# Layer 1 of a two-block transformer kernel: memory heads first, gate panels last, the gates' sigmoid from Exp, Ln and Exp

## The chip, the core and the metric

The kernel runs on one core of a Trainium2 chip. The metric is the device time of one execution in microseconds (us). Five engines work from queues of their own, each strictly in program order: TensorE (PE in the profile, with its weight loads as PEld), VectorE (DVE), ScalarE (ACT), GpSimd (POOL) and SyncE (SP), which issues the loads. They meet at semaphores: an instruction whose wait is not met holds up everything behind it on its engine.

## What is computed

Two blocks run one after the other on 256 tokens of width 1024. The first block has two layers; the change concerns the second of them, layer 1: differential attention over six heads, attention to a memory of 256 rows over four heads, a silu gate on each, and an output projection. All is float32.

```python
h = rms_norm(x, pre_norm[1])
mem_n = rms_norm(mem, mem_norm[1])
k_sh, v_sh = jnp.split(rms_norm(x, kv_norm) @ w_kv, 2, axis=-1)
proj = h @ b_w_in[0]
q, gate, q_mem, g_mem = jnp.split(proj, [BR_W, 2 * BR_W, 2 * BR_W + MEM_W], axis=-1)
# differential attention, per head of 2 x 64 (q, k) and 128 (v)
s = jnp.where(allowed, q @ k.T + bias, -jnp.inf)            # two score maps
attn = softmax(s)[0] - lam * softmax(s)[1]
y_br = rms_norm(attn @ v, subln) * (1.0 - lam_init)
# memory attention, four heads of 64
y_mem = softmax(q_mem @ k_mem.T * 64 ** -0.5) @ v_mem
y = jnp.concatenate([y_br * silu(gate), y_mem * silu(g_mem)], axis=-1) @ w_out[1]
x = x + rms_norm(y, post_norm[1])
```

Then the second block follows (a feed-forward, a mixer with retention and sparse attention, another feed-forward), which the change leaves as it is.

## The kernel before

Activations lie feature-major, in tiles of 128 features by 256 tokens. Weights stream from HBM in panels of 1024 x 128 (one output tile). For float32 accuracy each panel is split: ScalarE copies it to a rounded high part `wh` (step `w_hi`, L1684), VectorE subtracts to get the low part `wl` (step `w_lo`, L2058), and TensorE makes 24 matmuls of 256 columns (L2625, L2626, L2628: high by high, high by low, low by high, for eight slices of 128 features). The inputs are split in the same way into `xh` and `xl` (or `kh` and `kl`).

The function `schedule` makes one list of steps, and each engine's program walks that list and issues its own part of each step. So the order of the list is the order of every queue. `weight_order` fixes the order in which panels are loaded and used; up to five panels are split ahead of their use in this layer. `project` puts a panel's matmuls in the list and keeps its evacuation (for layer 1 the step `proj1` on VectorE, L2331, which multiplies the bank by the row norm and writes `qT`, `kT`, `qm1`, `gm1` or `gate1`) until after the next panel's matmuls; `settle` and `need` put it there at once.

Layer 1 has 28 panels before its output projection: six for q, six for the gate, two for the memory's query (`b_w_in` 12, 13), two for the memory's gate (14, 15), and twelve for k and v (`w_kv`). `LAYER1_BETWEEN` lists most of them in order, and `fill` takes the next one whenever an attention step leaves room. The attention itself is written as streams that `skewed` starts one behind the other:

- `diff_head(h)`, six of them. TensorE makes the scores (step `dif_s_mm`, L2928); VectorE adds the distance bias and takes maxima (`dif_s`, L2356 to L2360); ScalarE takes the Exp with its sums (L1931) and VectorE scales and combines the two maps (`dif_p`, L2366 to L2377); TensorE turns the result (`dif_t`, L2936) and ScalarE copies it; TensorE multiplies with the values (`dif_o`, L2943) and ScalarE squares it (L1943); TensorE sums the squares (`dif_n`, L2610), ScalarE takes Ln and Exp (L1669, L1671) and VectorE writes the head's output `rh` (L2384).
- `memory_stream(j)`, two of them, each with two heads: scores (`mem_s`, L2880), maxima on VectorE (`mem_a`, L2256, L2260), Exp on ScalarE (L1855), normalisation on VectorE (`mem_p`, L2266, L2270), turns on TensorE (`mem_b`, L2891) with copies on ScalarE (L1862), and the product with the values (`mem_c`, L2901), which VectorE multiplies with the gate (L2278).

Before the change the memory streams come after the six heads. The first of them also issues the gates: for the two `gm1` and the six `gate1` tiles ScalarE's Sigmoid (L1675, with a table load, L1662, ahead of it) and GpSimd's product with the gate itself (L1631). Then the step `branch` for each of the six tiles multiplies `rh` with the gate (VectorE, L2292), copies the high part (ScalarE, L1882) and subtracts the low part (VectorE, L2296); the output projection begins with these six slices for its first two panels (L2642 to L2646, `mm_group`), stops for `mem_c` and the two memory tiles, and ends with their two slices. `ln_tables` loads the table of Exp and Ln again. `mix_out` runs the other six panels; the first of them starts at L2625.

## Time and profile before

| | |
|---|---|
| median of three runs | 1252.0 us (1248.49 to 1253.15) |
| the profiled execution | 1251.89 us, of which its span is 1250.1 us |
| mean granted TensorE clock | 0.978 of full speed |
| TensorE busy | 1173.2 us, 94% of the span |
| VectorE, ScalarE, GpSimd busy | 68%, 50%, 15% |
| the chain that ended last | PE 81%, DVE 11%, ACT 5% |
| layer 1 in the span | from about 256 us to about 425 us |

All times below are us from the start of the span. A timeline row gives the start, the busy time, the engine, the line, what is written and read, and in brackets how long the engine sat idle before it and who released it. TensorE's matmuls are pipelined, so a row's time is longer than its distance to the next row. Operands named `bank` are in PSUM; `ta` holds constant tables, among them the identity for turns.

### The profile page before, as it was taken

The page shows a single profiled execution, that of the slowest core. Times are in us where ns is not written, and L with a number is a line of the kernel's source. Part 1 is how long each engine was busy: PE and PEld are TensorE (multiplying, and loading weights), DVE is VectorE, ACT ScalarE, POOL GpSimd, SP SyncE. Part 2 cuts the span into 40 slices and gives each one's busy share as a digit, 9 for nine tenths or more (in the row PEclk, how much of TensorE's full clock was granted, in tenths as well). Part 3 has the DMA queues.
Part 4 walks back from the last instruction along what each step waited for, and adds up shares of the span by engine and source line. Part 5 has one row for each costly group of instructions (what it writes and reads, how often), then busy time and mean ns, then how long its engine had stood idle before and what let it go on. Part 6 is the DMA issues. An engine that isn't in the chain of part 4 may idle for free.

```text
span 1250.1 us, 23926 instructions
## 1 busy us (share of the span) xinstructions
PE 1173.2 (94%) x9718; PEld 1126.7 (90%) x9718; DVE 844.0 (68%) x1448; ACT 626.9 (50%) x1076; POOL 184.4 (15%) x186
## 2 busy tenths in 40 slices
PE   6979699888997899999999999999999999999997
PEld 5978687788986899999989998999999999999997
DVE  6678854776776686665488755779556668877653
ACT  6765343664556554453343344653445445755542
POOL 1127130200002022110112000014100001122201
PEclk9999799999997899999999999999999999999999
DMA  7343211343452565556335542346454346766571
GB/s 258 126 135 116 83 57 35 121 146 122 136 169 84 180 219 172 183 143 193 120 110 195 170 161 79 115 139 188 163 175 162 136 137 198 233 209 197 161 214 36
DMA packets 53677, 186.83 MB, mean 149 GB/s; under 512 B 6720, under 2 KB 8896, under 8 KB 53184
## 3 DMA queue, kind: packets, MB, share of 16 engines
q1 hardware_dynamic: 53008, 183.07, 45.3%
q10 hardware_dynamic: 560, 2.24, 0.5%
q8 instruction: 77, 1.26, 0.4%
q14 instruction: 32, 0.26, 0.1%
HBM read 184.24 MB, written 1.05 MB: 148 GB/s over the span
## 4 chain that ended last, share of the span: by engine, by line
PE 81%; DVE 11%; ACT 5%; issue 2%; DMA 0%; POOL 0%; DVEq 0%; ACTq 0%
PE bank L2625 22%; PE bank L2628 21%; PE bank L2626 21%; DVE wl L2058 3%; PE bank L2642 2%; PE bank L2987 1%; PE bank L2643 1%; PE bank L2646 1%; PE bank L2665 1%; ACT wh L1684 1%; PE bank L2610 1%; DVE zl L2165 1%; PE bank L2674 1%; DVE sqr L2169 1%; PE bank L2785 1%
## 5 line engine op out<-in xcount | busy, mean ns | idle before, releaser
L2058 DVE TENSOR_TENSOR wl<-raw,wh 128x1024 fp32r<-128x1024 f32 (+1 forms) x343 | 423.1, 1243 | 189.6 <-ACT wh L1684 185.8
L1684 ACT ACTIVATE wh<-raw 128x1024 fp32r<-128x1024 f32 (+1 forms) x343 | 355.1, 1045 | 259.4 <-PE bank L2628 247.4
L2625 PE MATMUL bank<-x2h,wh 128*128 128x256 f32 (+1 forms) x1464 | 417.8, 285 | 0.9 <-ACT wh L1684 0.9
L2628 PE MATMUL bank<-x2h,wl 128*128 128x256 f32 (+1 forms) x1464 | 414.2, 283 | 2.8 <-DVE wl L2058 2.8
L2626 PE MATMUL bank<-x2l,wh 128*128 128x256 f32 (+1 forms) x1464 | 413.8, 283 | 0.0
L2628 PEld LDWEIGHTS bank<-x2h,wl 128*128 128x128 f32 x1464 | 276.2, 189 | 3.6 <-DVE wl L2058 3.6
L2625 PEld LDWEIGHTS bank<-x2h,wh 128*128 128x128 f32 x1464 | 276.0, 188 | 2.5 <-ACT wh L1684 1.1
L2626 PEld LDWEIGHTS bank<-x2l,wh 128*128 128x128 f32 x1464 | 276.7, 189 | 0.2
L2625 PE MATMUL bank<-xh,wh 128*128 128x256 f32 x416 | 122.6, 295 | 0.5 <-ACT wh L1684 0.2
L2628 PE MATMUL bank<-xh,wl 128*128 128x256 f32 x416 | 118.9, 286 | 4.2 <-DVE wl L2058 4.2
L2626 PE MATMUL bank<-xl,wh 128*128 128x256 f32 x416 | 118.3, 284 | 0.0
L2628 PE MATMUL bank<-hh,wl 128*128 128x272 f32 (+1 forms) x352 | 99.0, 281 | 0.0
L2625 PE MATMUL bank<-hh,wh 128*128 128x272 f32 (+1 forms) x352 | 99.0, 281 | 0.0
L2626 PE MATMUL bank<-hl,wh 128*128 128x272 f32 (+1 forms) x352 | 99.0, 281 | 0.0
L2628 PEld LDWEIGHTS bank<-xh,wl 128*128 128x128 f32 x416 | 81.3, 196 | 5.2 <-DVE wl L2058 5.2
L1636 POOL TENSOR_TENSOR hl<-tmp,hh 128x272 fp32r<-128x272 f32 (+1 forms) x44 | 53.4, 1213 | 218.8 <-ACT hh L1964 218.8
L2625 PEld LDWEIGHTS bank<-xh,wh 128*128 128x128 f32 x416 | 81.2, 195 | 4.3 <-issue 2.9
L2626 PEld LDWEIGHTS bank<-xl,wh 128*128 128x128 f32 x416 | 81.2, 195 | 0.2
L2050 DVE TENSOR_TENSOR tmp<-bank,rstd 128x256 f32<-128x256 f32 (+1 forms) x105 | 44.8, 428 | 35.3 <-PE bank L2628 35.3
L2625 PEld LDWEIGHTS bank<-hh,wh 128*128 128x128 f32 x352 | 66.2, 188 | 0.0
L2626 PEld LDWEIGHTS bank<-hl,wh 128*128 128x128 f32 x352 | 66.2, 188 | 0.0
L2628 PEld LDWEIGHTS bank<-hh,wl 128*128 128x128 f32 x352 | 66.2, 188 | 0.0
(393 smaller groups left out, 1942.9 us busy)
## 6 DMA issues: line engine op xcount, KB each, us to landing
raw<-w_ffn_gate SPq DMA_DIRECT2D x44, 512.0 KB, 4.1
raw<-w_ffn_up SPq DMA_DIRECT2D x44, 512.0 KB, 4.2
raw<-w_a_w_in SPq DMA_DIRECT2D x29, 512.0 KB, 3.6
raw<-w_ffn_down SPq DMA_DIRECT2D x32, 448.0 KB, 3.8
raw<-w_w_out SPq DMA_DIRECT2D x16, 512.0 KB, 3.5
raw<-w_b_w_in SPq DMA_DIRECT2D x16, 512.0 KB, 4.6
raw<-w_ffn_down SPq DMA_DIRECT2D x16, 512.0 KB, 3.9
raw<-w_ret SPq DMA_DIRECT2D x16, 512.0 KB, 3.6
```

Of the source, the lines that this page charges most:

```text
L1636: g.tensor_tensor(hid[n][1][:, panel, :], tmp2[t][:, 0:FFN_TOK[n]], hid[n][0][:, panel, :].bitcast(F32), ALU.subtract).then_inc(*f_lo.up(( ...
L1684: s.activation(splits[buf][0][:, 0:nk * P], raws[n % N_RAW][:, 0:nk * P], ACT.Copy).then_inc(*w_hi.up(n))
L2050: return v.tensor_tensor(out, banks[b][:, 0:n_tok], rstd[:, lo:lo + n_tok], ALU.mult)
L2058: v.tensor_tensor(lo[:, c], raws[n % N_RAW][:, c], hi[:, c].bitcast(F32), ALU.subtract).then_inc(*w_lo.up(n))
L2165: v.tensor_tensor(prod, lanes[:, 0:s, s:s + 1].broadcast_to([P, s, n]), lanes[:, s:s + 1, s + 1:BLK].broadcast_to([P, s, n]), ALU.mult).th ...
L2169: v.tensor_tensor(lanes[:, 0:s, s + 1:BLK], lanes[:, 0:s, s + 1:BLK], prod, ALU.add).then_inc(*ln.up(s))
L2610: last = pe.matmul(banks[b][:, 0:n_tok], tab(table), x, start=(k == 0), stop=(k == len(tiles) - 1))
L2625: pe.matmul(ps, hi[:, c], x_hi(k), start=(k == 0), stop=False)
L2626: pe.matmul(ps, hi[:, c], x_lo(k), start=False, stop=False)
L2628: last = pe.matmul(ps, lo[:, c], x_hi(k), start=False, stop=(k == kt - 1))
L2642: pe.matmul(ps, hi[:, c], x_hi(k), start=(first and k == part[0]), stop=False)
L2643: pe.matmul(ps, hi[:, c], x_lo(k), start=False, stop=False)
```

## The change

The two query panels of the memory are used first after `w_kv` panel 0, and the memory streams are started ahead of the six heads; only `mem_c` stays at the end. The gates' panels stay last, in the order gm, then gate. Each gate tile's sigmoid is issued right behind its evacuation, as three ScalarE instructions: Exp(-x), Ln(1 + e), Exp(-l). Exp and Ln are in one table set, so no table is loaded between. GpSimd's product follows as before. VectorE's product of a head with its gate (`branch_mul`) is issued as soon as both are in the list. The projection's first two panels then run in one piece, with the memory's slices first and head 5's slice last.

```diff
-LAYER1_BETWEEN = [pair for h in range(1, BT) for pair in (("b_w_in", h), ("w_kv", h), ("w_kv", BT + h - 1))
+LAYER1_BETWEEN = [("b_w_in", 12), ("b_w_in", 13)] + [pair for h in range(1, BT) for pair in (("b_w_in", h), ("w_kv", h), ("w_kv", BT + h - 1))
                   if pair not in (("b_w_in", 1), ("b_w_in", 2))] \
-    + [("w_kv", 2 * BT - 1)] + [("b_w_in", p) for p in list(range(12, 16)) + list(range(6, 12))]
+    + [("w_kv", 2 * BT - 1)] + [("b_w_in", p) for p in [14, 15] + list(range(6, 12))]
...
+            def gate_of(which, first_panel):
+                plain = scaled(which, first_panel)
+
+                def evac(panel, b, n):
+                    i = panel - first_panel
+                    freed_by = plain(panel, b, n)
+                    t, f_t = tmp.take()
+                    do("silu1", which, i, t, f_t)
+                    tmp.give(t, (sil1, (which, i)))
+                    for j in gates_done:
+                        if j in heads_done and j not in multiplied:
+                            multiply(j)
+                    if which == "gate":
+                        gates_done.append(i)
+                    return freed_by
+                return evac
...
                 for _ in range(3):
                     next(g)
-                    fill()
                     yield
-                if j == 0:
-                    need("b_w_in", 11)
-                    for which, n in (("gm", MT), ("gate", BT)):
-                        for i in range(n):
-                            t, f_t = tmp.take()
-                            do("silu1", which, i, t, f_t)
-                            tmp.give(t, (sil1, (which, i)))
                 memory_ends.append(g)
 
-            skewed([diff_head(h) for h in range(BT)] + [memory_stream(j) for j in range(MT)])
-            for i in range(BT):
-                do("branch", i)
-            begun = begin_out(1, range(BT))
+            skewed([memory_stream(j) for j in range(MT)] + [diff_head(h) for h in range(BT)])
+            need("b_w_in", 11)
             for g in memory_ends:
                 for _ in g:
                     pass
-            do("branch", BT)
-            do("branch", BT + 1)
+            order = [BT, BT + 1] + list(range(BT))
+            for i in order[:-1]:
+                if i < BT - 1 and i not in multiplied:
+                    multiply(i)
+                do("branch", i)
+            multiply(BT - 1)
+            do("branch", BT - 1)
+            begun = begin_out(1, order)
             do("ln_tables")
...
+                    key, s_t = ("1" + which, i), tmp1[t][:, :]
+                    tables(ACT.Exp)
                     on.wait_ge(*ev1.past((which, i)))
                     after(on, f_t)
-                    sigmoid(tmp1[t][:, :], buf[:, i, :], ("1" + which, i))
+                    s.activation(s_t, buf[:, i, :], ACT.Exp, scale=-1.0).then_inc(*sg_e.up(key))
+                    on.wait_ge(*sg_e.past(key))
+                    s.activation(s_t, s_t, ACT.Ln, bias=tab("ones")[:, 0:1]).then_inc(*sg_l.up(key))
+                    on.wait_ge(*sg_l.past(key))
+                    s.activation(s_t, s_t, ACT.Exp, scale=-1.0).then_inc(*sg.up(key))
```

VectorE's queue after the key copy of panel 0 (`kT`), before the change: head 0 comes at once (`scb0`, `stb0`), and two splits (`wl`) stand behind it.

```order
L2331 SCALAR_TENSOR_TENSOR kT<-bank6,rstd 128x256
L2356 SCALAR_TENSOR_TENSOR scb0<-ta,bank0 128x384
...
L2377 SCALAR_TENSOR_TENSOR scb0<-scb0,stb0 128x256
L2058 TENSOR_TENSOR wl0<-raw0,wh0 128x1024
L2058 TENSOR_TENSOR wl1<-raw1,wh1 128x1024
L2331 SCALAR_TENSOR_TENSOR kT<-bank3,rstd 128x256
```

The same place after the change, with the memory's statistics in `mst10`, `mst11` and its probabilities in `mp10` to `mp13`:

```order
L2356 SCALAR_TENSOR_TENSOR kT<-bank6,rstd 128x256
L2084 TENSOR_TENSOR wl0<-raw0,wh0 128x1024
L2356 SCALAR_TENSOR_TENSOR qm1<-bank0,rstd 128x256
...
L2296 TENSOR_SCALAR mp11<-mp11,mst10 128x256 x2
L2084 TENSOR_TENSOR wl1<-raw1,wh1 128x1024
L2356 SCALAR_TENSOR_TENSOR qm1<-bank5,rstd 128x256
...
L2296 TENSOR_SCALAR mp13<-mp13,mst11 128x256 x2
L2381 SCALAR_TENSOR_TENSOR scb0<-ta,bank0 128x384
```

The first pair's normalisation and a split now stand ahead of the second query's copy, and both pairs stand ahead of head 0.

ScalarE's queue around the turn of head 4 (`ptb10`), before the change: splits (`wh`) lie close behind each other.

```order
L1943 ACTIVATE tmp1<-bank2 128x256
L1684 ACTIVATE wh0_0<-raw1 128x1024
L1938 ACTIVATE ptb10<-bank4 128x384
L1684 ACTIVATE wh0_1<-raw2 128x1024
L1931 ACTIVATE scb2,stb1<-scb2,stb1 128x128
```

The same place after the change:

```order
L1979 ACTIVATE tmp2<-tmp2 128x256
L1963 ACTIVATE tmp3<-bank1 128x256
L1704 ACTIVATE wh2<-raw3 128x1024
L1958 ACTIVATE ptb10<-bank6 128x384
L1704 ACTIVATE wh0<-raw0 128x1024
L1975 ACTIVATE tmp1<-gate1 128x256
L1977 ACTIVATE tmp1<-tmp1,ta 128x256
L1979 ACTIVATE tmp1<-tmp1 128x256
L1975 ACTIVATE tmp2<-gate1 128x256
...
L1951 ACTIVATE scb2,stb1<-scb2,stb1 128x128
```

Six gate instructions now stand between the split and head 5's Exp, and six more (for gm) stand ahead of the square of head 3 (`tmp3<-bank1`).

VectorE's queue ahead of head 5, after the change (before it, the two copies were those of `gm1` and no product stood there):

```order
L2084 TENSOR_TENSOR wl2<-raw3,wh2 128x1024
L2356 SCALAR_TENSOR_TENSOR gate1<-bank4,rstd 128x256
L2356 SCALAR_TENSOR_TENSOR gate1<-bank0,rstd 128x256
L2316 TENSOR_TENSOR rh<-rh,gate1 128x256
L2381 SCALAR_TENSOR_TENSOR scb2<-ta,bank7 128x384
```

The product L2316 of head 0 with its gate, which waits for GpSimd, now stands ahead of head 5's scores.

## Rows read from the trace of the kernel before

**Rows 1.** The page, part 1: busy us, share of the span, instructions.
```profile
PE 1173.2 (94%) x9718; PEld 1126.7 (90%) x9718; DVE 844.0 (68%) x1448; ACT 626.9 (50%) x1076; POOL 184.4 (15%) x186
```

**Rows 2.** Waits of TensorE, 255 to 440 us: total, times, longest.
```profile
PE bank L2642 <- DVE xl L2296: 6.0, 2, 5.1
...
PE bank L2891 <- DVE mp L2270: 4.1, 1, 4.1
```

**Rows 3.** Timeline of TensorE: start, duration, engine, line, operands, count, [idle before].
```profile
280.84 1.65 PE L2928 MATMUL bank<-kT,qT 64*128 64x128 f32 x8
...
288.87 0.55 PE L2936 MATMUL bank<-ta,scb 128*128 128x128 f32 x3 [2.57 <-DVE scb L2377]
```

**Rows 4.** Timeline of VectorE: key copy, first differential head, two splits.
```profile
280.28 0.41 DVE L2331 SCALAR_TENSOR_TENSOR kT<-bank,rstd 128x256 f32<-128x256 f32 x1
282.49 0.55 DVE L2356 SCALAR_TENSOR_TENSOR scb<-ta,bank 128x384 f32<-128x384 f32 x1 [1.80 <-PE bank L2928]
...
288.33 0.48 DVE L2377 SCALAR_TENSOR_TENSOR scb<-scb,stb 128x256 f32<-128x256 f32 x1
288.74 2.35 DVE L2058 TENSOR_TENSOR wl<-raw,wh 128x1024 fp32r<-128x1024 f32 x2
```

**Rows 5.** Windows: length, PE, PEld, DVE, ACT, POOL busy, granted clock, DMA.
```profile
284.00:285.00 1.00, 1.00 (x10) 1.00 (x9) 0.93 (x4) 0.00 (x0) 0.00 (x0) 0.90 0.11 45
...
376.00:377.00 1.00, 0.00 (x0) 0.00 (x0) 0.00 (x0) 0.97 (x5) 0.00 (x0) 0.68 0.00 0
...
389.00:390.00 1.00, 1.00 (x7) 1.00 (x6) 1.00 (x2) 0.62 (x1) 0.00 (x0) 0.50 0.00 0
...
417.00:418.00 1.00, 0.00 (x0) 0.00 (x0) 0.96 (x3) 0.63 (x2) 0.00 (x0) 0.66 0.88 348
...
424.00:425.00 1.00, 1.00 (x9) 1.00 (x8) 0.00 (x0) 1.00 (x4) 0.00 (x0) 0.93 0.41 74
```

**Rows 6.** Timeline of all engines: second memory pair, gates, output projection.
```profile
371.58 1.14 DVE L2270 TENSOR_SCALAR mp<-mp,mst 128x256 f32<-128x256 f32 x4
...
371.64 1.13 PE L2880 MATMUL bank<-kmT,qm 64*128 64x256 f32 x8
...
372.82 1.29 DVE L2256 TENSOR_REDUCE mst<-bank 128x2 f32<-128x512 f32 x2
...
374.34 0.47 ACT L1855 ACTIVATE mp<-bank,mst 128x256 f32<-128x256 f32 x1 [2.22 <-DVE mst L2260]
...
376.06 0.21 ACT L1855 ACTIVATION_READ_ACCUMULATOR mp<-bank,mst 128x1 f32 x1
...
378.07 1.28 ACT L1662 ACT_TABLE_LOAD   x1
...
378.39 1.97 PE L2891 MATMUL bank<-ta,mp 128*128 128x128 f32 x8 [4.12 <-DVE mp L2270]
...
379.86 1.41 POOL L1631 TENSOR_TENSOR gm<-gm,tmp 128x256 f32<-128x256 f32 x2 [133.64 <-ACT tmp L1675]
...
385.49 0.55 PE L2642 MATMUL bank<-xh,wh 128*128 128x256 f32 x1 [5.13 <-DVE xl L2296]
```

**Rows 7.** Timeline of ScalarE: a head's Ln and Exp, then a split.
```profile
342.12 0.45 ACT L1669 ACTIVATE tmp<-bank,consts 128x256 f32<-128x256 f32 x1
342.60 0.42 ACT L1671 ACTIVATE tmp<-tmp 128x256 f32<-128x256 f32 x1
342.93 1.05 ACT L1684 ACTIVATE wh<-raw 128x1024 fp32r<-128x1024 f32 x1
```

**Rows 8.** Timeline of VectorE: two projection copies; last head's probabilities done.
```profile
345.76 0.74 DVE L2331 SCALAR_TENSOR_TENSOR qm<-bank,rstd 128x256 f32<-128x256 f32 x2
...
356.12 0.48 DVE L2377 SCALAR_TENSOR_TENSOR scb<-scb,stb 128x256 f32<-128x256 f32 x1
```

**Rows 9.** Timeline of TensorE: last head's scores and turn, last value turn.
```profile
349.32 0.93 PE L2928 MATMUL bank<-kT,qT 64*128 64x128 f32 x8
...
353.02 0.59 PE L2610 MATMUL bank<-tmp,ta 128*128 128x256 f32 x2
...
359.59 0.49 PE L2936 MATMUL bank<-ta,scb 128*128 128x128 f32 x3
...
369.93 0.38 PE L2674 MATMUL bank<-ta,tmp 128*128 128x128 f32 x2
```

**Rows 10.** Timeline of TensorE: memory outputs, then the first plain output panel.
```profile
391.93 1.95 PE L2901 MATMUL bank<-mpt,vm 128*64 128x256 f32 x16
...
396.22 0.28 PE L2625 MATMUL bank<-xh,wh 128*128 128x256 f32 x1
```

**Rows 11.** Timelines of VectorE and GpSimd: a split beside an addition.
```profile
400.96 1.52 DVE L2058 TENSOR_TENSOR wl<-raw,wh 128x1024 fp32r<-128x1024 f32 x1
...
400.67 0.73 POOL L1583 TENSOR_TENSOR sq<-sq 128x256 f32<-128x256 f32 x1 [1.10 <-ACT sq L1889]
```

More of the change, by code:

```diff
@@ L525, in build @@
         mo_sq, mo_y, mo_s, mo_x = (signal(n) for n in ("mix_sq", "mix_y", "mix_scaled", "mix_x"))
-        ev1, sil1 = signal("proj1"), signal("silu1")
+        ev1, sil1, sg_e, sg_l = (signal(n) for n in ("proj1", "silu1", "gate_exp", "gate_log"))
         lam_a, lam_mm, lam_e, lam_d, lam, sub_d = (signal(n) for n in (
@@ L1111, in scaled, with multiply @@
                 return evac
-            q_evac, k_evac, g_evac = scaled("q", 0), scaled("k", 0), scaled("gate", 6)
-            qm_evac, gm_evac = scaled("qm", 12), scaled("gm", 14)
+            heads_done, gates_done, multiplied = [], [], []
+            def multiply(i):
+                do("branch_mul", i)
+                multiplied.append(i)
+            def gate_of(which, first_panel):
[13 more added lines that the diff above has]
+                return evac
+            q_evac, k_evac, g_evac = scaled("q", 0), scaled("k", 0), gate_of("gate", 6)
+            qm_evac, gm_evac = scaled("qm", 12), gate_of("gm", 14)
             v_evac, flush = token_major("v1", S)
@@ L1165, in diff_head @@
                 tmp.give(r, (d_r, h))
+                heads_done.append(h)
                 fill()
@@ L2285, in vector_program @@
                                     xh[:, c, :].bitcast(F32), ALU.subtract).then_inc(*in_lo.up(("y0", j)))
[L2286 to L2297 removed]
+                elif kind == "branch_mul":
+                    i, = a
+                    on.wait_ge(*d_r.past(i))
+                    on.wait_ge(*sil1.past(("gate", i)))
+                    v.tensor_tensor(rh1[:, i, :], rh1[:, i, :], gate1[:, i, :], ALU.mult).then_inc(*branch.up(i))
+                elif kind == "branch":
+                    k, = a
+                    on.wait_ge(*used.past(LAST_PRE1))
+                    on.wait_ge(*in_hi.past(("y1", k)))
+                    v.tensor_tensor(xl[:, k, :], rh1[:, k, :] if k < BT else qm1[:, k - BT, :],
+                                    xh[:, k, :].bitcast(F32), ALU.subtract).then_inc(*in_lo.up(("y1", k)))
                 elif kind == "mo_evac":
```

10 lines of the change are left out of this document (removed).

## The prediction

> **What bounds the kernel now.** I read the page first: TensorE is busy for 94% of the span [rows 1], so the time falls only where TensorE waits or runs at a low clock. Then I read its waits in layer 1. The largest stand at the layer's end: 6.0 us for the low parts of the projection's input and 4.1 us for the normalised memory probabilities [rows 2]. Last I read the timelines at the two places where the change puts its work. At the end TensorE starts the projection at 385.49 after 5.13 us idle, and the turns of the memory's second pair at 378.39 after 4.12 us [rows 6]. At the start of the attention there is one wait, 2.57 us ahead of head 0's turn at 288.87 [rows 3]. The windows give the granted clock: 0.50 is 1.2 GHz, 1.00 is 2.4 GHz. It fell in the window of 376 (0.68), when TensorE had been idle since 374.3, and was still at 0.50 in the window of 389; it had fallen in the window of 417 as well, and was up again in that of 424 [rows 5]. At the low clock the same eight score matmuls took 1.65 us instead of 0.93 [rows 3, 9], a factor of 1.77.
>
> I lay out the changed queues at both ends. **A panel costs TensorE** some 2.8 us: from 349.32 to 359.59 lie three panels, 0.9 of scores, 0.6 of a norm sum and 0.5 of a product [rows 9]. A split is 1.15 us on VectorE (half of 2.35) and 0.95 on ScalarE, whose next instruction follows that soon [rows 4, 7].
>
> **Start of the attention.** Until 280.84 both kernels do the same. There the old one makes the scores of head 0; the new one uses the first memory query panel. The clock is low until about 284.1 (0.90 in the window of 284) [rows 5], so that panel costs 2.8 + 1.4 and ends at 285.2. VectorE's copy is 0.4 and TensorE's scores are 1.13 [rows 4, 6]: 286.9. Then a chain that TensorE has to wait for, from the old second pair [rows 6]:
> - maxima to first Exp 1.5 (372.82 to 374.34), four Exps 1.9 (to 376.27), reciprocal and normalisation 0.2 + 1.15: 4.8 us, to 291.7;
> - a split that stands ahead of the second query's copy, 1.15, and the copy 0.4: 293.3.
>
> TensorE has the second query panel beside it, to 289.7, and waits 3.6 us. I take the clock to fall in this wait, since 4.1 us of idleness ahead of 378.39 did that. The second scores then take 2.0, to 295.3. Behind them VectorE has the same chain of 4.8 (300.1) and then head 0, which took 6.3 us from 282.49 to 288.81 [rows 4]: 306.5 with the hops. TensorE has turns (1.97 at the low clock [rows 6]), scores, one panel and the other turns beside that, to 302.5, and waits 4.0 us. So head 0's turn moves from 288.87 to 306.5, which is 17.6 us. The clock is low again; after 385.49 it took some 4.4 us to rise [rows 5, 6], and 4 us at a factor of 1.77 lose 1.7. The stretch behind starts **19.3 us later**. Only some 10.1 of it is work that is moved here (two panels 5.7, scores 2.3, turns 2.1). The rest, 9.2, is new waiting. If the clock stays high in both waits it is 16.8; if it rises later, 20.5.
>
> From here to head 5's scores (old: 349.32) both have 20 panels and the same heads, and TensorE had no long wait there; I cost it at nothing. That is covered only while the panels are split in time, five ahead.
>
> **End of the layer.** I count from head 5's scores as zero. Head 5's turn was at 10.27, and its probabilities were ready at 356.60, which is 7.3: 3.0 us of cover [rows 8, 9]. Now a gate's sigmoid costs ScalarE 0.48 + 0.48 + 0.33, about 1.3 us (an activation starts 0.48 after the one it depends on, and the next free one 0.33 later [rows 7]).
> - The two copies that stood at 345.76 [rows 8], which is -3.6, are now those of gm; their sigmoids hold ScalarE from -3.1 to -0.5. The split behind them is done at 0.7 instead of about -4, so VectorE's split ends at 1.9 and gate 0's copy at 2.3.
> - Gate 0: sigmoid 1.35, GpSimd 0.75 (half of 1.41 [rows 6]), and VectorE's product, for which head 5 stands and waits: 4.9. Head 5's 6.3 end at 11.2. TensorE waits 1.0 where it had 3.0 of cover, and its last panel ends at 15.1.
> - VectorE goes on with split, head 3, split, gates 2 and 3: 14.9. ScalarE has their sigmoids until 16.8; then product, split, split behind ScalarE's split, gate 4's copy: 19.7. Sigmoid 21.0, Ln and Exp of head 4 22.0, head 4 and gate 5's copy 22.8, sigmoid 24.2.
> - Only then comes ScalarE's copy of the last value turn, for which TensorE stands at head 5's product: 24.5. Product 25.4, square, norm sum, Ln and Exp 27.6. The memory's products take 1.95 at the high clock [rows 10] and 3.5 at the low one: from 26.6 to 30.1. Gate product 0.4, high part 0.4, first low part: the projection starts at 31.0.
> - It has 48 matmuls, as two panels 5.7 us, and some 1.1 for the low clock: the first plain panel starts at 37.7.
>
> Before, it started at 396.22 [rows 10], which is 46.9. Of the 9.2 us between, 10.1 is again the moved work, so this end waits about 1 us more than before: the two table loads of 1.28 us [rows 6] and the long wait for the gates go, and a queue of gates ahead of head 5 comes. TensorE is through with its last panel at 15.1, and from there to 31.0 it has under 5 us of work. The old kernel stood from 369.93 to 385.49 [rows 6, 9].
>
> **Sum.** +19.3 - 9.2 = +10.1 us. The profiled execution took 1251.89 us, 0.1 from the median of 1252.0; the changed kernel should take 1262. Behind the layer nothing is changed: the loads were ahead, and TensorE's wait for the next block's input stays.
>
> **The rivals.**
> - *The gates fit beside the panels*, and ScalarE does not fall behind. Then the last panel ends at 13.9, and head 4's norm, gate 5's sigmoid, the value copy, head 5 and the memory products follow in 9.1 us, plus 6.7 for the projection's first two panels: 29.7 instead of 37.7. That is 1254, not slower than can be told. For it: ScalarE is busy for only 50% of the span [rows 1]. Against it: in the eight gate panels (22.7 us and some 4 of small work) ScalarE has eight splits of 0.95, eight sigmoids of 1.3 and the heads, about 26 us, each piece behind a wait.
> - *The memory's chain hides at the start*: TensorE finds its 8 us there. Then only the gain at the end stands, 9.2 less 1 for hops: 1244. Against it: the copy of the second query stands behind the chain in VectorE's queue, and there is one panel beside it. It decides from a chain under 2.8 us, and the rows give 6.4.
> - *GpSimd slows VectorE in the gate stretch.* A split took 1.52 us beside an addition of 0.73 on GpSimd, against 1.2 otherwise [rows 4, 11]. Eight gate products at 0.3 are 2.4 us, of which a part is on the path. If each held VectorE for its whole 0.75, it would be 6 us, and the time 1268.
>
> The Trainium skill (SBUF — State Buffer, "Who interferes with whom") says that a VectorE instruction with two SBUF inputs and a GpSimd one that reads SBUF exclude each other: the second "fully blocks". By that rule the third rival holds in full; the row of 1.52 shows a good 0.3 for one overlap, which may be a partial one.
>
> **How the numbers follow.** That the gates are issued without table loads is seen in the new order, so that is no rival. My forecast (1258.5 to 1266.5) has 0.60. The first rival has 0.17, within 0.5% of before, as 0.5% (6.3 us, up to 1258.3) is about what a measurement of this kernel can tell from no change. The second has 0.07. The third, or a clock that stays low longer, has 0.16. So faster is 0.07, same 0.17, slower 0.76. The bounds: the start at 16.8 takes 2.5 off and at 20.5 adds 1.2, and the end may be off by 3 either way; with the first and third rival this gives 1253 to 1268.
>
> **What the changed profile would show.** At the start: waits of TensorE of about 3.6 us ahead of the second memory scores and 4.0 ahead of head 0's turn, released by VectorE, with the granted clock at 0.50 behind them. Head 0's turn at about 306. Head 5's scores at about 368.6, with its turn a further 11.3 behind. No table load on ScalarE in the layer. Some 9 us of idleness ahead of the last head's product, released by ScalarE's value copy, and the first plain output panel at about 406. I would be wrong if head 0's turn came before 300, or if the last value copy followed its turn within 2 us.

## The result, and the profile after

The changed kernel takes 1264.5 us (median of 6 runs, 1263.5 to 1267.9), the kernel before on the same chip 1252.6 us (6 runs, 1248.3 to 1258.3). The ratio is 1.0094, with a 95% interval of 1.0067 to 1.0120: slower by 12 us. The forecast was 1262.0. The profiled execution took 1265.09 us, of which its span is 1263.3.

The page of the changed kernel, part 1 (busy us, share of the span, instructions), answers to [rows 1]:

```profile
PE 1179.9 (93%) x9718; PEld 1132.1 (90%) x9718; DVE 843.2 (67%) x1448; ACT 631.2 (50%) x1090; POOL 182.6 (14%) x186
```

TensorE has the same instructions and is busy for a smaller share of a longer span. TensorE's waits between 255 and 455 us (total, times, longest) answer to [rows 2]:

```profile
PE bank L2968 <- issue: 6.8, 1, 6.8
PE bank L2961 <- DVE scb L2402: 6.5, 2, 5.5
...
PE bank L2905 <- DVE qm L2356: 4.0, 2, 3.5
...
PE bank L2667 <- DVE xl L2321: 1.0, 1, 1.0
```

The wait for the projection's input fell from 6.0 to 1.0 us and that of 4.1 us ahead of the memory's turns is gone. In their place stand three others: 4.0 us for the memory's queries (L2356), 6.5 us for heads' probabilities (L2402), and 6.8 us ahead of the last head's product (L2968), which the view calls "issue".

To size layer 1 alone I use two marks that both kernels have: the last value turns of the memory (`tmp`, with a wait of 1.03 us just behind), ahead of all that was changed, and the wait of 4.54 us for the next block's input, behind it. TensorE's timelines, first before, then after:

```profile
278.95 0.44 PE L2674 MATMUL bank<-ta,tmp 128*128 128x128 f32 x2 [0.82 <-DVE tmp L2089]
...
418.54 0.57 PE L2642 MATMUL bank<-x2h,wh 128*128 128x272 f32 x1 [4.54 <-DVE x2l L2318]
```

```profile
283.26 0.44 PE L2699 MATMUL bank<-ta,tmp 128*128 128x128 f32 x2 [0.82 <-DVE tmp L2115]
...
429.96 0.56 PE L2667 MATMUL bank<-x2h,wh 128*128 128x272 f32 x1 [4.54 <-DVE x2l L2343]
```

Two things are to be seen. Between the marks lie 139.6 us before and 146.7 after, so the layer is 7.1 us longer. And the first mark is itself 4.3 us later, in a part of the program that the change doesn't touch. The windows between the marks (length; busy us of TensorE and its loads, VectorE, ScalarE, GpSimd; granted clock; DMA) say of what kind the 7.1 us are:

```profile
278.95:418.54 139.59, 119.06 (x941) 110.93 (x941) 94.94 (x189) 73.94 (x164) 9.76 (x13) 0.93 0.41 131
```

```profile
283.26:429.96 146.70, 118.01 (x940) 108.75 (x941) 93.34 (x189) 78.07 (x178) 10.42 (x13) 0.95 0.37 125
```

TensorE's busy time is about the same (119.1 and 118.0 us). Its idle time went from 20.5 to 28.7 us. In this pair of profiles the whole loss in the layer is new waiting.

The starts of the attention and of its end in TensorE's timeline of the changed kernel, for [rows 3, 9, 10]:

```profile
295.97 1.13 PE L2905 MATMUL bank<-kmT,qm 64*128 64x256 f32 x8 [3.47 <-DVE qm L2356]
...
308.29 0.90 PE L2961 MATMUL bank<-ta,scb 128*128 128x128 f32 x3 [5.49 <-DVE scb L2402]
...
369.90 0.93 PE L2953 MATMUL bank<-kT,qT 64*128 64x128 f32 x8
...
381.32 0.55 PE L2961 MATMUL bank<-ta,scb 128*128 128x128 f32 x3 [0.99 <-DVE scb L2402]
...
395.01 1.19 PE L2968 MATMUL bank<-ptb,vt 128*128 128x256 f32 x2 [6.77 <-issue]
...
402.11 0.36 PE L2667 MATMUL bank<-xh,wh 128*128 128x256 f32 x1 [0.95 <-DVE xl L2321]
...
407.64 0.28 PE L2650 MATMUL bank<-xh,wh 128*128 128x256 f32 x1
```

Both waits for the memory's chain are there (3.47 and 5.49 us), and so is the wait at the last head's product (6.77 us). The timelines of VectorE, ScalarE and GpSimd show what that last one waits for:

```profile
386.54 0.42 DVE L2316 TENSOR_TENSOR rh<-rh,gate 128x256 f32<-128x256 f32 x1 [1.61 <-POOL gate L1651]
386.88 1.22 DVE L2084 TENSOR_TENSOR wl<-raw,wh 128x1024 fp32r<-128x1024 f32 x1
...
388.25 1.52 DVE L2084 TENSOR_TENSOR wl<-raw,wh 128x1024 fp32r<-128x1024 f32 x1
...
392.39 0.48 DVE L2409 SCALAR_TENSOR_TENSOR rh<-bank,small,tmp 128x256 f32<-128x256 f32 x1 [1.95 <-ACT tmp L1691]
392.79 0.41 DVE L2356 SCALAR_TENSOR_TENSOR gate<-bank,rstd 128x256 f32<-128x256 f32 x1
```

```profile
393.24 0.42 ACT L1975 ACTIVATE tmp<-gate 128x256 f32<-128x256 f32 x1 [0.88 <-DVE gate L2356]
...
394.55 0.37 ACT L1733 ACTIVATE vt<-bank 128x256 f32<-128x256 f32 x1
```

```profile
387.08 1.61 POOL L1651 TENSOR_TENSOR gate<-gate,tmp 128x256 f32<-128x256 f32 x1 [0.57 <-ACT tmp L1979]
```

ScalarE's copy of the last values (`vt`, 394.55) stands behind gate 5's sigmoid, which waited 0.88 us for VectorE's copy of gate 5 (392.79). That copy stands behind head 4's output (392.39), for which VectorE had waited 1.95 us for ScalarE's Exp of the norm (L1691), and this in turn comes behind the other gates, their sigmoids and the splits. So the two engines wait for each other by turns.

### The profile page after: what moved, and what is told of

It reads as the page before. It is cut to its first block, busy times and chain, and to the rows that moved or that the text cites. A ratio compares the mean times of both kernels' runs of the same rounds, so it can differ in the third digit from the quotient of the medians.

```text
span 1263.3 us, 23943 instructions
## 1 busy us (share of the span) xinstructions
PE 1179.9 (93%) x9718; PEld 1132.1 (90%) x9718; DVE 843.2 (67%) x1448; ACT 631.2 (50%) x1090; POOL 182.6 (14%) x186
## 4 chain that ended last, share of the span: by engine, by line
PE 77%; DVE 14%; ACT 6%; issue 2%; DMA 0%; DVEq 0%; POOL 0%; ACTq 0%; POOLq 0%
PE bank L2650 21%; PE bank L2653 20%; PE bank L2651 20%; DVE wl L2084 4%; PE bank L3012 1%; PE bank L2667 1%; ACT wh L1704 1%; PE bank L2671 1%; PE bank L2668 1%; PE bank L2690 1%; PE bank L2635 1%; DVE sqr L2195 1%; DVE zl L2191 1%; PE bank L2699 1%; ACT scb L1951 1%
```

## The experiments

Between the two marks every kernel has the same work for TensorE, so this table holds what the profiles say, beside the times. Two profiles of one kernel differ by 1.2 us (before) and 0.8 us (changed) in the stretch, and the part behind the second mark takes between 830.0 and 833.8 us in all profiles, without an order that I can see. So a microsecond or two of a difference can come from chance. "First mark" is its time in the profile, idle is the stretch less TensorE's busy time, the clock is the granted one in the stretch.

| kernel | median us | ratio to before (95%) | first mark | stretch | TensorE busy | idle | clock |
|---|---|---|---|---|---|---|---|
| before | 1252.6 | | 278.95 | 139.6 | 119.1 | 20.5 | 0.93 |
| before, second profile | 1249.8 (one run) | | 278.79 | 138.4 | 116.8 | 21.6 | 0.95 |
| changed | 1264.5 | 1.0094 (1.0067 to 1.0120) | 283.26 | 146.7 | 118.0 | 28.7 | 0.95 |
| changed, again | 1263.7 | 1.0085 (1.0055 to 1.0115) | 282.82 | 147.5 | 118.9 | 28.6 | 0.95 |
| memory first alone | 1260.8 | 1.0064 (1.0044 to 1.0085) | 278.70 | 145.3 | 118.1 | 27.2 | 0.95 |
| gates' half alone | 1259.9 | 1.0054 (1.0032 to 1.0076) | 280.43 | 146.6 | 122.7 | 24.0 | 0.91 |
| changed, panels back | 1253.2 | 1.0010 (0.9989 to 1.0031) | 281.97 | 140.2 | 120.5 | 19.7 | 0.92 |
| two of them kept | 1262.5 | 1.0075 (1.0050 to 1.0101) | 280.43 | 148.1 | 123.8 | 24.3 | 0.92 |
| changed, late products | 1260.8 | 1.0068 (1.0044 to 1.0091) | 282.35 | 148.0 | 123.1 | 24.8 | 0.92 |
| changed, one Exp | 1261.1 | 1.0051 (1.0020 to 1.0081) | 278.87 | 145.7 | 123.0 | 22.7 | 0.91 |
| panels back, late products | 1250.6 | 0.9980 (0.9960 to 1.0001) | 281.10 | 136.9 | 119.7 | 17.2 | 0.93 |
| woven | 1249.0 | 0.9965 (0.9937 to 0.9993) | 279.74 | 134.6 | 119.1 | 15.4 | 0.96 |
| woven, late splits | 1246.8 | 0.9943 (0.9918 to 0.9968) | 280.50 | 132.3 | 118.0 | 14.4 | 0.97 |
| woven, late sigmoids too | 1245.0 | 0.9912 (0.9882 to 0.9942) | 280.02 | 132.6 | 118.2 | 14.4 | 0.97 |

The runs were made on several chips, each beside the kernel before on the same one (1252.6 to 1255.7 us). So kernels of different chips are compared by their ratios. The kernel with one Exp leaves out two instructions of each gate's sigmoid; it computes another function, and only its times are of use.

### The memory first, without the gates' half

This and the next kernel each do one half of the change. In this one the block of the gates' Sigmoids (with its table loads) comes as a whole behind the heads, and the memory's slices end the projection, as before.

```diff
-LAYER1_BETWEEN = [pair for h in range(1, BT) ...
+LAYER1_BETWEEN = [("b_w_in", 12), ("b_w_in", 13)] + [pair for h in range(1, BT) ...
...
                 for _ in range(3):
                     next(g)
-                    fill()
                     yield
...
-            skewed([diff_head(h) for h in range(BT)] + [memory_stream(j) for j in range(MT)])
+            skewed([memory_stream(j) for j in range(MT)] + [diff_head(h) for h in range(BT)])
```

> The half of the change that puts the memory heads first; the gates stay as before (one Sigmoid each with a table load, in one block behind the heads, the memory slices last in the projection). My theory (new waits at the start of the attention, about 9 us, are the loss of the change, and the end gives little back): both new waits of TensorE stand here too (3.5 ahead of the second memory scores, 5.5 ahead of head 0's turn), head 5's scores come 16 us later than before counted from the value turns, and from them the first plain output panel follows in about 34 us (37.7 in the changed kernel, 46.9 before). Sum +4 us: 1256.5. Rival theory (the gates' three activations on ScalarE are the loss): without them this half is faster than before, 1245 to 1250.

Measured: 1260.8 us, above both. The start has the waits of the changed kernel to a hundredth: 3.48 us ahead of the second scores (291.40) and 5.49 ahead of head 0's turn. At the end the projection still waits for its input behind the block of gates (TensorE's timeline):

```profile
303.71 0.90 PE L2934 MATMUL bank<-ta,scb 128*128 128x128 f32 x3 [5.49 <-DVE scb L2375]
...
390.47 0.55 PE L2640 MATMUL bank<-xh,wh 128*128 128x256 f32 x1 [7.69 <-DVE xl L2294]
```

What follows: putting the memory first loses 5.7 us of the stretch by itself. The start came as expected: head 5's scores are 16.3 us later than before, counted from the mark. I had expected +4 in the time, and two things were missed. From head 5's scores the first plain output panel follows in 36.2 us and not in 34, and 2.2 us of the loss of the profiled execution lie behind the second mark.

### The gates' half, with the old order of panels

```diff
-LAYER1_BETWEEN = [("b_w_in", 12), ("b_w_in", 13)] + [pair for h in range(1, BT) ...
+LAYER1_BETWEEN = [pair for h in range(1, BT) ...
...
-    + [("w_kv", 2 * BT - 1)] + [("b_w_in", p) for p in [14, 15] + list(range(6, 12))]
+    + [("w_kv", 2 * BT - 1)] + [("b_w_in", p) for p in list(range(12, 16)) + list(range(6, 12))]
...
-            skewed([memory_stream(j) for j in range(MT)] + [diff_head(h) for h in range(BT)])
+            skewed([diff_head(h) for h in range(BT)] + [memory_stream(j) for j in range(MT)])
```

> The other half alone: each gate's sigmoid from Exp, Ln and Exp behind its panel and its product with the head as soon as possible, but the memory heads last as before. My theory: nothing changes at the start of the attention; the wait of 5.1 us ahead of the projection goes down to 1 or 2 us, ScalarE falls behind by 1 to 3 us in the gate panels; sum -1 to -4 us, 1249 to 1251.5. Rival theory (the gates on ScalarE are the loss): 1258 or more, with head 5's turn waiting for VectorE.

Measured: 1259.9 us, the rival's number. I had expected a gain of 1 to 4 us. The rival's mechanism, a wait for VectorE ahead of head 5's turn, isn't there: that turn (361.40) has no wait of note. Neither the start nor the heads moved: head 0's turn is 9.9 us behind the mark, as before. The loss is in one place, seen in the timelines of TensorE, ScalarE and VectorE:

```profile
380.14 1.22 PE L2968 MATMUL bank<-ptb,vt 128*128 128x256 f32 x2 [8.02 <-ACT vt L1733]
```

```profile
379.40 0.42 ACT L1979 ACTIVATE tmp<-tmp 128x256 f32<-128x256 f32 x1
379.72 0.36 ACT L1733 ACTIVATE vt<-bank 128x256 f32<-128x256 f32 x1
```

```profile
363.70 0.43 DVE L2316 TENSOR_TENSOR rh<-rh,gate 128x256 f32<-128x256 f32 x1 [1.96 <-POOL gate L1651]
...
369.55 0.42 DVE L2316 TENSOR_TENSOR rh<-rh,gate 128x256 f32<-128x256 f32 x1 [1.62 <-POOL gate L1651]
...
379.43 0.43 DVE L2316 TENSOR_TENSOR rh<-rh,gate 128x256 f32<-128x256 f32 x1 [1.68 <-POOL gate L1651]
```

TensorE stands 8.02 us at the last head's product for ScalarE's value copy (379.72), the instruction behind gate 5's sigmoid, as in the changed kernel. The two table loads of 1.28 us [rows 6] are gone, but VectorE waits three times for GpSimd with everything else queued behind (1.96, 1.62 and 1.68 us), and the granted clock in the stretch falls from 0.93 to 0.91, with which TensorE's busy time grows by 3.6 us for the same work. From head 4's turn to the second mark it is 72.4 us before and 79.1 here; with the memory first it is 61.7 without the gates' half and 63.2 with it. So each half loses by itself (5.7 and 7.0 us of the stretch), but the gates' half costs 6.7 us where the memory's steps still stand at the end and 1.5 where they don't.

### The panels back between the memory's steps

```diff
                 for _ in range(3):
                     next(g)
+                    fill()
                     yield
```

> The changed kernel with one line back: a weight panel is put behind each of the three steps of a memory stream, so that TensorE has work while VectorE and ScalarE make the memory's softmax. My theory: the waits of 3.5 and 5.5 us at the start go (under 1 us each); six panels are then used up earlier, so head 5 has no panels beside its softmax and the end waits some 3 to 5 us more; sum 1255 to 1260, 4 to 9 us under the changed kernel. Rival theory (the waits at the start do not matter since the end sets the time by ScalarE's queue): within 2 us of the changed kernel.

Measured: 1253.2 us, below the theory's range, and the same as before. This shows the cause of the loss at the start: with one weight panel beside each of the memory's steps, the wait ahead of the second scores is 0.76 us instead of 3.47, and there is none ahead of head 0's turn. A new wait stands at the other end, where panels are now short (TensorE's timeline):

```profile
296.26 1.13 PE L2906 MATMUL bank<-kmT,qm 64*128 64x256 f32 x8 [0.76 <-DVE qm L2357]
...
382.91 0.90 PE L2962 MATMUL bank<-ta,scb 128*128 128x128 f32 x3 [7.21 <-DVE scb L2403]
```

### Two of these panels kept for the end

```diff
-                for _ in range(3):
+                for step in range(3):
                     next(g)
-                    fill()
+                    if j == 0 or step == 0:
+                        fill()
                     yield
```

> The kernel with the panels back between the memory's steps, but two of the five kept for the end: a panel beside each of the first four steps only. Theory: the start needs only 9 us of cover, 3.2 panels, so its waits stay under 2 us in all, and the two panels that are left (5.7 us) stand in TensorE's wait of 7.2 us ahead of head 5's turn: 1248.5 to 1251. Rival: where the panels stand does not matter, since the memory's products, the gates and the last head hold the end by VectorE and ScalarE; head 5's turn comes as late and the time stays at 1252.5 to 1256.

Measured: 1262.5 us, 9 us above the kernel with all panels back (8 by the ratios). The theory failed. The wait ahead of head 5's turn did shrink, from 7.21 to 4.08 us, but others came: 2.53 us ahead of head 0's turn, 3.08 us in front of value turns in mid-stretch, and 5.45 us ahead of head 4's norm sum (TensorE's timeline, then ScalarE's):

```profile
349.96 0.44 PE L2701 MATMUL bank<-ta,tmp 128*128 128x128 f32 x2 [3.08 <-DVE tmp L2117]
...
383.59 0.55 PE L2963 MATMUL bank<-ta,scb 128*128 128x128 f32 x3 [4.08 <-DVE scb L2404]
...
389.59 1.22 PE L2637 MATMUL bank<-tmp,ta 128*128 128x256 f32 x2 [5.45 <-ACT tmp L1965]
```

```profile
389.18 0.37 ACT L1965 ACTIVATE tmp<-bank 128x256 f32<-128x256 f32 x1
```

Head 4's square (389.18) stands behind the sigmoids of gates 4 and 5, because the two kept panels are gates' panels, and each brings a VectorE copy and a sigmoid into the queues just where the last heads need them. A gate's panel is poor cover for a wait at the end. That is not the whole of the 7.9 us in the stretch: the waits at the start and in the middle came back too, and 3.3 us are busy time of TensorE. What made the wait in the middle, beyond its release by VectorE, isn't shown.

### The late products, twice

VectorE's products of heads 0 to 4 with their gates, issued together ahead of the last head's norm, in the changed kernel and in the one with the panels back:

```diff
-                    for j in gates_done:
-                        if j in heads_done and j not in multiplied:
-                            multiply(j)
...
+                if h == BT - 1:
+                    need("b_w_in", 11)
+                    for i in range(BT - 1):
+                        multiply(i)
                 do("dif_n", h, t, r, f_r, ob, b, freed)
```

> The changed kernel, but VectorE's products of heads 0 to 4 with their gates are issued together ahead of the last head's norm, where VectorE waits for ScalarE anyway, instead of each behind a gate's panel. Theory: these products make VectorE wait for GpSimd (up to 2 us each) with head 5, the splits and the gates' own copies queued behind, and this feeds back to ScalarE's sigmoids. Then the last gate's sigmoid and the last value copy (7 us of idleness of TensorE) come 2 to 4 us earlier: 1260.5 to 1262.5. Rival: what is late is ScalarE's own work (three instructions for each gate and the splits); the waits only move, and the time stays within 1 us of 1264.5.

> The same late products, but in the kernel that has the panels back between the memory's steps (1253.18). There TensorE waits 7.2 us ahead of head 5's turn, and VectorE had waited twice for GpSimd, 1.95 and 1.68 us, in the 22 us before. Theory as for the other one: head 5's turn 2 to 3.5 us earlier against head 5's scores, 1250 to 1251.5. Rival: VectorE's two splits and ScalarE's queue are what head 5 stands behind, and the time stays at 1252.5 to 1254.

Measured: with the panels back 1250.6 us, in the range of the theory. That is 2.6 below 1253.2, but on two chips; the ratios are 0.9980 and 1.0010, and their intervals overlap. The stretch is 3.3 us shorter. Head 5's turn came only 1.1 us earlier against its scores (10.5 us behind them instead of 11.6), where the theory had 2 to 3.5; from head 4's turn to the projection's start it is 24.5 us instead of 26.4.

In the changed kernel it is 1260.8 us by the median (1.0068 against 1.0094 and 1.0085, again with overlapping intervals). At the end the theory holds: against head 5's scores the last head's product starts at 22.4 us instead of 25.1, and the projection at 29.6 instead of 32.2. The stretch of the profile is not shorter even so: 4 us of idle time went, and 4 to 5 us of TensorE's busy time came, with the clock at 0.92 instead of 0.95. The windows of 20 us at the start of the attention show where (changed kernel, then this one):

```profile
284.00:304.00 20.00, 14.08 (x114) 12.20 (x114) 11.51 (x29) 7.64 (x23) 0.00 (x0) 1.00 0.32 111
```

```profile
284.00:304.00 20.00, 16.00 (x106) 13.90 (x106) 9.78 (x25) 7.12 (x21) 0.00 (x0) 0.83 0.29 100
```

So counted from head 4's turn the projection starts 1.9 and 2.6 us earlier when VectorE doesn't wait for GpSimd in the gates' stretch. In the changed kernel's profile the low clock at the start took this back, and a gain in the time isn't shown beyond the noise in either.

### One Exp in place of the sigmoid

```diff
                     s.activation(s_t, buf[:, i, :], ACT.Exp, scale=-1.0).then_inc(...)
-                    s.activation(s_t, s_t, ACT.Ln, bias=tab("ones")[:, 0:1]).then_inc(...)
-                    s.activation(s_t, s_t, ACT.Exp, scale=-1.0).then_inc(...)
```

> The changed kernel with only the first of the three ScalarE instructions of each gate's sigmoid (its output is Exp(-x) times the gate, so the Ln and the second Exp are left out). It measures what ScalarE's queue costs in the gate stretch: 0.9 us less for each of eight gates. Theory: the last value copy waits for ScalarE's queue of sigmoids, each behind VectorE's copy; the projection starts 3 to 4.5 us earlier against head 5's scores (32.2 in the changed kernel): 1260 to 1261.5. Rival: VectorE's splits, head 5 and the waits for GpSimd hold the end; the projection starts under 1.5 us earlier: 1263 to 1264.5.

Measured: 1261.1 us. TensorE's timeline around the last head's product and the projection:

```profile
387.05 1.19 PE L2964 MATMUL bank<-ptb,vt 128*128 128x256 f32 x2 [5.42 <-issue]
...
394.93 0.55 PE L2663 MATMUL bank<-xh,wh 128*128 128x256 f32 x1 [0.95 <-DVE xl L2317]
```

From head 4's turn to the projection's start it is 31.3 us, where the changed kernel has 35.4: 4.05 us earlier, within the 3 to 4.5 of the theory. Against head 5's scores it is the same gain (28.15 instead of 32.21 us). So ScalarE's queue of sigmoids is on the path to the last value copy. It is not all of it: 5.42 us of the 6.77 are still there. The stretch is only 1.0 us shorter than in the changed kernel's first profile, since here the granted clock was 0.91 and TensorE was busy 5 us longer.

### The changed kernel again

> The changed kernel once more, unaltered. In its first profile layer 0, which the change does not touch, ended 4.3 us later than in the kernel before (the value turns at 283.26 instead of 278.95), in steps at which the granted clock was 0.91 instead of 1.00 for a window of 20 us. If that is a matter of the single execution, these turns come at 279 to 285 in this one and layer 1 alone (from those turns to the wait for the next block's input) is again 146 to 147.5 us, against 139.6 before; the median stays at 1264 to 1266. If it goes with the program, the turns stand at 283 again.

> The kernel before once more, for a second profile. In the first profiles the changed kernel reached the value turns of layer 1, ahead of anything that the change touches, 4.3 us later than the kernel before. If that is a matter of the single execution, this profile will lie elsewhere than 278.95 us, by a microsecond or more; if it belongs to the change, it lies at 278.95 within 0.5.

Measured: 1263.7 us, with the first mark at 282.82 and the stretch at 147.5; the kernel before has it at 278.79 and 138.4 in its second profile. So the layer's loss is 7.1 us in one pair of profiles and 9.1 in the other, and the 4 us at the first mark came back in both. By the conditions written ahead of these two runs they belong to the program and not to the single execution. The kernel with one Exp speaks against that: up to the mark it has the changed kernel's instructions and loads, and it reached the mark at 278.87.

### A version below both kernels

The lesson of the kernels with the panels back is that TensorE should have something else than gates' panels at the end. In the woven kernel the memory's products, the two memory tiles and heads 0 to 2 come ahead of head 5's turn, and the projection begins with these five slices:

```diff
+                if h == BT - 1:
+                    for g in memory_ends:
+                        for _ in g:
+                            pass
+                    for i in range(3):
+                        multiply(i)
+                    for i in [BT, BT + 1] + list(range(3)):
+                        do("branch", i)
                 pt, f_pt = ptb_ring.take()
                 b, freed = bank.take()
                 do("dif_t", h, pb, pt, f_pt, b, freed)
...
                 if h == BT - 1:
                     flush()
+                    begun.append(begin_out(1, [BT, BT + 1] + list(range(3))))
...
-                    for i in range(BT - 1):
+                    for i in range(3, BT - 1):
                         multiply(i)
+                        do("branch", i)
                 do("dif_n", h, t, r, f_r, ob, b, freed)
```

> The kernel with the panels back and the products late (1250.59), and the end woven anew: the memory's products, the branches of both memory tiles and of heads 0 to 2 come ahead of head 5's turn in the list, the projection's first two panels begin with these five slices ahead of head 5's product, heads 3 and 4 follow ahead of its norm. Theory: TensorE's 6.85 us ahead of head 5's turn and its 6 us of short waits and low clock behind are places where work that has long been ready (3.4 us of memory products at the low clock, 30 of the projection's 48 matmuls) can stand, while head 5's own chain stays. The projection then ends 4 to 8 us earlier: 1243 to 1247. Rival: VectorE and ScalarE, with five branches and three splits now between head 5's steps, make head 5 later by what TensorE gains: 1249 to 1252.

The next two move rows of the finished list: the ScalarE half of the split of `w_out1` panel 3 and the VectorE half of panel 2 to behind the last value turn, and then also the sigmoids of gates 4 and 5 (`silu1`) to behind `dif_p` of head 5.

> As the woven one, and two halves of splits for output panels (ScalarE's for panel 3, VectorE's for panel 2) moved from ahead of head 5's chain to behind its turn. Theory: head 5's maxima started 3.1 us after its scores were done, behind these halves and two copies, so head 5's turn comes 2 to 3 us earlier and the time is 1 to 3 us below the woven one. Rival: the halves are then late for the output panels, or VectorE's copies of gates 4 and 5 hold head 5 anyway, and it is the same within 1 us.

> The woven kernel with late splits (1246.82), and the sigmoids of the last two gates moved on ScalarE from ahead of head 5's four Exps to behind them. Theory: these Exps waited 1.8 us for the sigmoids (VectorE was idle 3.60 us for them where it is 1.93 elsewhere), TensorE waits 3.46 us ahead of head 5's turn, and the gates' products are needed last; so the turn comes 1.5 to 1.8 us earlier and the time is 1245 to 1246. Rival: the norm of head 3, which stands behind the sigmoids on ScalarE, now holds VectorE's queue ahead of the memory's products, and the projection starts no earlier: 1246.5 to 1247.5.

Measured: 1249.0, 1246.8 and 1245.0 us (ratios 0.9965, 0.9943, 0.9912). The woven one came out 2 us above its range, at the edge of the rival's, but below before: head 5's turn comes no earlier behind head 4's than in the kernel with late products (13.7 us in both), so what was gained is the work that now stands in its wait. TensorE's and VectorE's rows of the one with late splits:

```profile
371.95 1.95 PE L2931 MATMUL bank<-mpt,vm 128*64 128x256 f32 x16
...
377.36 0.77 PE L2966 MATMUL bank<-ta,scb 128*128 128x128 f32 x3 [3.46 <-DVE scb L2407]
...
379.84 0.55 PE L2672 MATMUL bank<-xh,wh 128*128 128x256 f32 x1 [0.43 <-DVE xl L2326]
```

```profile
369.30 0.55 DVE L2386 SCALAR_TENSOR_TENSOR scb<-ta,bank 128x384 f32<-128x384 f32 x1 [0.42 <-PE bank L2958]
...
375.42 0.18 DVE L2398 RECIPROCAL stb<-stb 128x4 f32<-128x4 f32 x1 [3.60 <-ACT scb L1956]
```

The memory's products take 1.95 us at the high clock in the gap where TensorE used to stand, and head 5's maxima start 0.95 us behind TensorE's first score matmul (368.35), where it was 4.2 in the kernel with late products. Then VectorE stands 3.60 us for the Exps, which are behind the two sigmoids. With these moved too, the turn comes 10.95 us behind head 4's instead of 12.17, but the projection's last part isn't earlier, for two reasons (TensorE's and VectorE's rows):

```profile
374.10 0.55 PE L2970 MATMUL bank<-ta,scb 128*128 128x128 f32 x3 [2.23 <-DVE scb L2411]
...
377.74 0.55 PE L2676 MATMUL bank<-xh,wh 128*128 128x256 f32 x1 [1.23 <-DVE xl L2330]
...
383.98 0.59 PE L2977 MATMUL bank<-ptb,vt 128*128 128x256 f32 x2
```

```profile
385.55 0.43 DVE L2330 TENSOR_TENSOR xl<-rh,xh 128x256 fp32r<-128x256 f32 x1 [2.40 <-ACT xh L1911]
```

The 30 matmuls of the five slices, from 377.74, last until 383.98 at the low clock (they took 4.0 us, to 383.87, in the kernel with late splits), and head 3's low part waits 2.40 us for ScalarE, whose copy is queued behind the last head's square. In the stretch the two are equal (132.3 and 132.6 us), and the intervals of their ratios overlap. Whether the last step gains anything is open. That the woven kernels with late splits are faster than before is not: 0.57% (0.32 to 0.82) and 0.88% (0.58 to 1.18).

## Why the prediction was right, and where not

The time came out 2.5 us above the forecast and inside the range, and most steps were met. But the layer lost less than the forecast said, and a part of the 12 us that no term stood for made up for it. That the number is so close is partly luck.

**Start of the attention: right mechanism, 3 us too large.** The two waits came where they were put, released by VectorE: 3.47 us (3.6 forecast) and 5.49 us (4.0). Head 0's turn is 15.1 us later than before if the 4.3 us at the first mark are taken off, and head 5's scores 16.3 us; the forecast said 17.6 and 19.3. The term that was mis-sized is the clock. I had it low in the first query panel and from the second scores on. In the windows it was 1.00 from 284 to 304, so the first panel had no 1.4 us on it, the second scores took 1.13 us and not 2.0, and TensorE was through earlier ahead of head 0's turn and waited longer. Behind that second wait it did fall:

```profile
308.00:312.00 4.00, 3.71 (x20) 3.71 (x21) 2.84 (x4) 1.66 (x3) 0.00 (x0) 0.57 0.35 122
```

I had given 16.8 for a clock that stays high in both waits. The 16.3 come from another case: it fell behind the second wait, and the first panel's 1.4, which stand in the 16.8 too, were missing. They were read from one profile of before, in which head 0's scores at 280.84 took 1.65 us. In the second profile of that kernel the clock was high there:

```profile
280.67 0.93 PE L2928 MATMUL bank<-kT,qT 64*128 64x128 f32 x8
```

**Between: 1.2 us.** From head 0's turn to head 5's scores the changed kernel is 1.2 us longer than before (61.6 and 60.5 us). The forecast had 1.7 us there for the low clock and nothing for waits, which fits.

**End of the layer: right to a tenth, partly by two errors that cancel.** From head 5's scores (369.90) to the first plain output panel (407.64) are 37.7 us, as forecast. Inside, VectorE's first product was at 4.7 (4.9), TensorE waited 0.99 us ahead of head 5's turn (1.0), the last value copy came at 24.7 (24.5). The 9 us of idleness ahead of the last head's product came in two parts, 2.09 us ahead of head 4's norm sum (387.32) and 6.77. The projection started at 32.2, where I had 31.0, but at the high clock, so that its two panels took 5.5 us and not 6.7. The kernel with one Exp shows that the queue of sigmoids is on this path, as the working had it.

**The sum: +10.1 for the layer, measured +7.1 and +9.1** in two pairs of profiles: the start +16.3 and the end -9.2 in the first, +17.3 and -8.2 in the second, against +19.3 and -9.2. The rest of the 12 us lies outside. In both pairs 4 us are there when layer 1 begins. Behind the second mark lie 1.8 us more in the first pair and 0.6 less in the second. The prediction has the sentence "Until 280.84 both kernels do the same", which is true of the instructions and not of the time. That term was missing, and what makes it is open.

**The rivals.** *The gates fit beside the panels* didn't happen: the last value copy waits for them. *The memory's chain hides* didn't either, but the kernel with the panels back shows that the price was the missing panels, not the chain: with one panel beside each step the start's waits go, and the time is that of before. I had written "there is one panel beside it" and taken that as given. *GpSimd slows VectorE* is there and small. Two splits beside GpSimd's product (386.88 and 388.25) took 2.89 us together, where two alone took 2.35 [rows 4], and that product 1.61 us, where others take 0.73. The Trainium skill (SBUF — State Buffer, "Who interferes with whom") has the second of such a pair fully blocked. The rows agree: the first split, already running, kept its 1.22 us, the product begun behind it ended 0.88 us late, at 388.69, and the second split ended 1.08 us after that. The split of [rows 11] also ended 1.08 us behind GpSimd's addition (402.48 and 401.40), so its 0.3 us fit a full exclusion, not a partial one, of two instructions that overlapped for 0.44 us. What keeps the price small is the number of meetings: only one of the eight products met splits. What VectorE did lose to GpSimd is waiting: 1.96 and 1.61 us in the order of its own queue. Much of such a wait is ScalarE's: in the first the sigmoid was done 1.1 us into the wait (373.75), and the product took 0.73.

## What to carry to other kernels

What a chain between engines costs depends on the work that stands beside it, so before moving one ahead, count the independent work that goes with it; here the panels between the memory's steps were worth 6.5 to 7.3 us in the layer and 9 to 11 in the time. Work put at the end as cover must not feed the queues on which the end depends: gates' panels there made it worse, while products and slices whose inputs had long been ready made it better. And an in-order engine that waits for the result of a slow path (VectorE for GpSimd's product) should do so last; here that brought the projection's start forward by 1.9 and 2.6 us.

## What was not expected of the hardware

**Identical work at other times.** Up to the first mark all engines have the same instructions, operands and waits in both kernels, apart from which weights a few late loads bring. Yet the mark stands at 278.95 and 278.79 in two profiles of before and at 283.26 and 282.82 in two of the changed kernel, and between 278.70 and 282.35 in the experiments. The offset grows in steps at which the granted clock differs (windows of 20 us, before, then after):

```profile
20.00:40.00 20.00, 17.59 (x132) 15.67 (x131) 14.11 (x31) 17.52 (x36) 4.31 (x7) 1.00 0.40 129
...
160.00:180.00 20.00, 18.03 (x190) 17.02 (x186) 7.09 (x12) 10.00 (x18) 9.16 (x11) 0.91 0.21 72
```

```profile
20.00:40.00 20.00, 17.60 (x119) 15.70 (x118) 14.26 (x30) 16.11 (x31) 4.34 (x7) 0.91 0.31 106
...
160.00:180.00 20.00, 18.02 (x215) 17.08 (x213) 7.30 (x12) 8.80 (x15) 7.64 (x9) 0.83 0.24 80
```

The second profile of before also had 0.91 in the first of these windows and came out at 278.79, having made it up by 180 us. What decides whether the clock falls in such a window I can't say from these profiles. The 4 us can't come from the instructions and loads ahead of the mark alone, since the kernel with one Exp has the same ones and reached it at 278.87. Whether they belong to the program in another way or to chance stays open.

**The same wait, another clock.** At the start of the attention the clock stayed at 1.00 behind a wait of 3.47 us in the changed kernel (the scores behind it took 1.13 us), while the windows of the kernel with late products show 0.83 from 284 to 304 about a wait of 3.48 us (these scores took 1.33). Behind the second wait it fell in both: 0.91 and 0.83 from 304 to 324, although the wait was 5.49 us in the first and 4.02 in the second. Between the marks TensorE was busy 4 to 5 us longer for the same work in the kernel with late products. So the length of a wait alone doesn't tell what the clock will cost behind it.
